# Six weight transfers per turn of an expert loop issued from ScalarE's queue instead of SyncE's

## What is computed

```python
def expert_block(args):                  # for every expert, on its tokens
    tok, e = args
    hdn = x_pad[tok] @ w1[e] + b1[e]     # 1024 -> 2 x 1024
    glu, lin = hdn[:, :D_FF], hdn[:, D_FF:]
    glu = jnp.minimum(glu, SWIGLU_LIMIT)
    lin = jnp.clip(lin, -SWIGLU_LIMIT, SWIGLU_LIMIT)
    act = glu * jax.nn.sigmoid(SWIGLU_ALPHA * glu) * (lin + 1.0)
    return act @ w2[e] + b2[e]           # 1024 -> 1024
```

## Time and profile before

| | us |
|---|---|
| median of 3 runs | 1288.67 |
| span of the profiled execution (first to last instruction) | 1287.6 |
| TensorE matmuls busy | 1224.8 (95%) |
| VectorE busy | 400.2 (31%) |
| ScalarE busy | 183.7 (14%) |
| GpSimd busy | 133.5 (10%) |

### The profile page before, as it was taken

One profiled execution on the slowest core, in us unless ns is written; L12 is line 12 of the kernel. 1 busy time (PEld: TensorE's weight loads), 2 busy tenths in 40 slices (PEclk: granted clock), 3 DMA queues, 4 the chain that ended last, 5 costly groups with the idle time before them and its releaser, 6 DMA issues.

```text
span 1287.6 us, 19010 instructions
## 1 busy us (share of the span) xinstructions
PE 1224.8 (95%) x8094; PEld 678.7 (53%) x8094; DVE 400.2 (31%) x876; ACT 183.7 (14%) x364; POOL 133.5 (10%) x125
## 2 busy tenths in 40 slices
PE   9999999999999999999999999989898989989896
PEld 8888889999864344434444443434243333324341
DVE  3869683575532121121212212021111202120213
ACT  1441621110031011101000110101010010101011
POOL 1000035788200000000000000000000000000001
PEclk9999999999999999999999999999899999999998
DMA  7745327367899999999999999999999999999995
GB/s 272 228 137 168 128 99 293 122 224 284 326 385 422 417 429 426 425 426 426 429 421 420 425 429 421 427 428 424 427 427 429 422 429 429 429 423 428 430 424 238
DMA packets 54561, 463.37 MB, mean 360 GB/s; under 512 B 12321, under 2 KB 14273, under 8 KB 19457
## 3 DMA queue, kind: packets, MB, share of 16 engines
q1 hardware_dynamic: 48576, 459.99, 87.2%
q10 hardware_dynamic: 5920, 2.45, 0.7%
HBM read 460.56 MB, written 1.87 MB: 359 GB/s over the span
## 4 chain that ended last, share of the span: by engine, by line
PE 62%; DMA 21%; SPq 3%; POOL 1%; DVE 1%; issue 1%; ACT 0%; POOLq 0%; DVEq 0%
PE ps L1215 27%; DMA mix<-expert_w 11%; DMA ring<-expert_w 10%; PE ps L1235 8%; PE ps L717 8%; PE ps L1122 4%; PE ps L1104 4%; SPq L591 3%; PE ps L740 2%; PE ps L1017 2%; PE ps L751 1%; DMA mix<-stream_w 1%; PE ps L1224 1%; PE ps L841 1%; PE ps L1208 1%
## 5 line engine op out<-in xcount | busy, mean ns | idle before, releaser
L1215 PE MATMUL ps<-ring,mix 128*64 128x512 f32 x1504 | 339.7, 596 | 8.8 <-DMA ring<-expert_w 8.7
L1215 PEld LDWEIGHTS ps<-ring,mix 128*64 128x64 f32 x1504 | 105.1, 137 | 200.4 <-issue 180.2
L1235 PE MATMUL ps<-ring,mix 128*64 128x512 f32 x752 | 172.0, 595 | 16.5 <-DMA ring<-expert_w 16.5
L1215 PE MATMUL ps<-mix 128*64 128x512 f32 x544 | 130.9, 624 | 13.2 <-DMA mix<-expert_w 13.2
L740 PE MATMUL ps<-mix 128*128 128x256 f32 x624 | 136.8, 380 | 0.0
L2244 DVE TENSOR_SCALAR mix<-ps 128x512 f32<-128x512 f32 x32 | 22.1, 691 | 353.7 <-PE ps L1215 353.7
L740 PEld LDWEIGHTS ps<-mix 128*128 128x128 f32 x624 | 117.9, 190 | 17.0 <-issue 1.2
L1235 PEld LDWEIGHTS ps<-ring,mix 128*64 128x64 f32 x752 | 51.8, 137 | 119.9 <-issue 85.4
L679 POOL TENSOR_TENSOR mix<-mix 128x1024 f32<-128x1024 f32 (+1 forms) x2 | 3.4, 1700 | 949.2 <-ACT mix L1651 949.2
L717 PE MATMUL ps<-mix 128*128 128x128 f32 x792 | 97.0, 276 | 0.3 <-POOL mix L651 0.3
L717 PEld LDWEIGHTS ps<-mix 128*128 128x128 f32 x792 | 92.1, 192 | 1.1 <-POOL mix L651 0.5
(11 more groups left out here) (297 smaller groups left out, 986.5 us busy)
## 6 DMA issues: line engine op xcount, KB each, us to landing
ring<-expert_w SPq DMA_DIRECT2D x106, 2048.0 KB, 30.5
mix<-expert_w SPq DMA_DIRECT2D x39, 2048.0 KB, 27.1
ring<-expert_w SPq DMA_DIRECT2D x70, 1024.0 KB, 24.9
mix<-stream_w SPq DMA_DIRECT2D x42, 1024.0 KB, 5.0
mix<-expert_w SPq DMA_DIRECT2D x15, 1024.0 KB, 13.9
mix<-expert_w SPq DMA_DIRECT2D x18, 512.0 KB, 24.6
mix<-stream_w SPq DMA_DIRECT2D x8, 512.0 KB, 4.3
mix<-first_w SPq DMA_DIRECT2D x4, 512.0 KB, 4.9
```

The lines of the kernel that those rows point to most:

```text
L1215: ins = mm(PS[64 * a:64 * a + 64, bank + g, :], XE[j][:, c, 64 * a:64 * a + 64], w[2 * a + g], start=start, stop=(c == KD - 1), skip_group ...
L1235: ins = mm(PS[64 * a:64 * a + 64, bank + h, :], HT[:, c // 4, c % 4, 64 * a:64 * a + 64], w[2 * h + a], start=(c == 0), stop=(c == KF - 1) ...
```

## The change

In the turns that run as a loop SyncE leaves out steps 9, 11, 13, 15, 17 and 19, and ScalarE issues them on its own queue: 9 and 11 behind the first sigmoid of the turn's first pair, 13 and 15 behind the second, 17 and 19 behind the copy of the left half. Each has the same wait on `chunk_used` as before, the same place and the same semaphore. ScalarE's loop is split like SyncE's, into one over turns 4 to 7 and one, under an If, for further rounds, since a transfer needs the number of the turn within its round. The turns that are written out are not changed.

```diff
+ACT_STEPS = ((9, 11), (13, 15), (17, 19))
@@ SyncE, load_turn
+                    if not isinstance(turn, int) and n in sum(ACT_STEPS, ()):
+                        continue
@@ ScalarE
+            def load_behind(turn, pair, part):
+
+                for n in ACT_STEPS[part]:
+                    act.wait_ge(E("chunk_used"), turn * PB * EC + STEPS * (n - SLOTS + 1))
+                    src = expert_w[bass.ds(pair + n // (EC // STEPS), 1), n % (EC // STEPS)].rearrange("e p n -> p (e n)")
+                    act.dma_start(PLACES[(n - AHEAD) % SLOTS], src).then_inc(E(f"steps_in{(n - AHEAD) % SLOTS}"), 16)
+
-            def turn_act(turn):
+            def turn_act(turn, pair=None):
                 for j in range(PB):
...
                     for f in range(2):
                         act.wait_ge(E("glu_ready"), 2 * i + f + 1)
                         A(SIG, GLU, ACT.Sigmoid, scale=SWIGLU).then_inc(E("sig_ready"), 1)
+                        if pair is not None and j == 0:
+                            load_behind(turn, pair, f)
...
                     nc_s.copy(YS[:, 0:512], PS[:, one, :]).then_inc(E("ys_left"), 1)
+                    if pair is not None and j == 0:
+                        load_behind(turn, pair, 2)
...
-            with act.Fori(STATIC, rounds * (NPAIR // PB)) as turn:
-                turn_act(turn)
+            with act.Fori(STATIC, NPAIR // PB) as q:
+                turn_act(q, q * PB)
+            with act.If(rounds > 1):
+                with act.Fori(1, rounds) as r:
+                    with act.Fori(0, NPAIR // PB) as q:
+                        turn_act(r * (NPAIR // PB) + q, q * PB)
```

## The result

Over ten executions each the changed kernel took 1291.47 us (median, 1290.71 to 1295.32) and the kernel before 1289.98 us (1288.41 to 1290.55). The ratio is 1.0018, with a 95% interval of 1.0009 to 1.0026: some 2.3 us slower, by 1.2 to 3.4 us (the two medians alone are 1.5 us apart). The forecast was +1.9.

What follows compares the result with a forecast made beforehand. DMA bytes bound the loop at 427 GB/s; even sharing of two queues ends TensorE's last turn at 115.8 us against 113.9, so 1288.67 + 1.9 = 1290.6 us. The range was 1286.0 to 1299.0.

Steps and rivals of the forecast that it cites:

- A2: Issue of steps 13 and 15 by ScalarE, 0.9 us after block 7's end, put at 48.6 us into the turn.
- Rival 1: DMA service of the two queues by whole blocks (+0.9 us, 1289.6) or in order of arrival (0); chance 0.15.
- the sum: Last turn: delayed blocks and clock loss make TensorE end at 115.8 us against 113.9, +1.9 us, thus 1290.6.
- the bound without the loss: Last turn without clock loss after waits: second issue at 46.9, block 12 at 66.7, end 117.5 us, +3.6 us.
- the floor of 114.8: Least end of the last turn, from block 8 landing at 49.0 us: 64.0 + 50.8 = 114.8, +0.9 us.
- rival 2: Two queues change the DMA rate: loss priced at 2%, 4.7 us, 1295.3, chance 0.20; gain 3.3 us, 1287.3, chance 0.08.
- Rival 3: SP's queue is the true brake in the loop; a shorter one gives back 10 us, 1280; chance 0.07.

## Why the prediction was right

**The bound.** Bytes bound the loop, as read from the share of 1.01: rate, turn length and the start of the last turn did not move. That lateness counts only in the last turn, as the prediction had it, is what the run with the change in turns 4 to 6 shows (0.9997).

**Issue times.** ScalarE's first issue in the last turn was 22.3 us into it (22.0 predicted), the second sigmoid 48.8 (A2 = 48.6). An issue took 0.344 us and not 0.32, and went out 0.2 us after the sigmoid had started and not 0.01. The address and the wait are worked out in between from the turn's number: in the run with the change in turn 7 only, where that number is a constant, the issue came 0.01 us behind the sigmoid (1184.94 against 1184.93). Nothing waited for it: behind its loop ScalarE still idles 2.08 us before its first activation, as in the earlier trace rows.

**Sharing.** An even share from 4 us after the issue was a choice made on exp_b alone; blocks 6, 7, 9, 11, 8 and 12 were put at 32.8, 42.6, 35.8, 45.6, 49.0 and 65.0 and came at 32.9, 42.7, 35.9, 45.7, 49.0 and 64.8. Rival 1 had 6 at 34.3, 7 at 44.1 and 9 at 29.4; if whole blocks alternated only from 4 us after the issue, block 6, then being moved, would have landed at 29.4 and block 9 at 34.3, which does not fit either. So rival 1 falls, and with it the reading of the Trainium skill (DMA: Bandwidth & Descriptors, Queues, rings and completion order) by which a turn between queues is as long as a whole block. That the queues take turns, as that section says, agrees with the trace. The queues' rows say something of packets after all: the 24 blocks added 3456 packets to q10 (9376 against 5920), which is 144 a block or 9 on each of the 16 engines. If the queues alternate by such packets, a turn is a ninth of a block, and that cannot be told from an even share; that they alternate so was not measured.

**The clock.** Behind the first of the two waits 16 matmuls took 5.18 us to the next start (1193.02 to 1198.20), 1.75 more than at full clock, and behind the second the row has the same 5.35; 1.7 was added for each. The granted clock agrees (columns as in the earlier trace rows): 0.83 in both stretches, so in part of each it was the lower of its two levels, 1.2 GHz and not 2.4.

```profile
1190.00:1200.00 10.00, 6.22 (x32) 2.40 (x32) 0.69 (x1) 0.00 (x0) 0.00 (x0) 0.83 1.00 428
1200.00:1210.00 10.00, 6.30 (x22) 1.93 (x24) 1.69 (x3) 0.63 (x1) 0.00 (x0) 0.83 1.01 429
```

Turn 6 of the same trace went otherwise. Block 6 lost 2.96 us (6.39 to the next start), so the wait for block 7 was only 2.35 us and block 7 ran at full speed; block 8 lost 1.5. What the sum depends on is block 7, and so this turn shows the bound without the loss:

```profile
1042.17 3.65 PE L1218 MATMUL ps<-mix 128*64 128x512 f32 x16 [0.98 <-DMA mix<-expert_w]
...
1074.60 6.57 PE L1218 MATMUL ps<-ring,mix 128*64 128x512 f32 x16 [3.81 <-DMA ring<-expert_w]
1080.99 1.04 PE L1227 MATMUL ps<-mix 128*64 128x128 f32 x16
1084.38 3.65 PE L1218 MATMUL ps<-mix 128*64 128x512 f32 x16 [2.35 <-DMA mix<-expert_w]
...
1108.86 3.65 PE L1218 MATMUL ps<-ring,mix 128*64 128x512 f32 x16 [0.95 <-DMA ring<-expert_w]
```

The second sigmoid started at 1088.81, T = 46.6 (46.9 in that bound), and block 12 came at 66.7 (66.7). A faster TensorE there makes ScalarE issue sooner and the pair end later. If the last turn of an execution goes like turn 6, it ends 2 us later; that would suit the wider spread of the changed kernel (4.6 us against 2.1), but is only argued. That this term came out right was in part luck. The prediction took 1.7 from one wait; in the same trace the wait of 3.37 us at 923.47 was followed by 6.35 us to the next start, 2.9 more than at full clock. By the prediction's own working such a loss at block 7 would have ended the turn at the floor of 114.8 (an estimate), and no loss at 117.5.

**The rivals.** No loss or gain of rate (rival 2): 428 to 431 GB/s in the first 80 us of the last turn and 422 in the next 20, where the kernel before has 419 to 433 over the same 100 us. Rival 3: SP's issue stalls did shrink, as this row of tile expert_w shows against the earlier trace rows, and gave nothing back; the Trainium skill's rule that spreading transfers over issuing engines does not help bandwidth (same page, Rules for kernel authors) holds here, with 427 GB/s before and after.

```profile
L594 SPq DMA_DIRECT2D mix<-expert_w x24: 327/594/4242, 443.5 to 1248.2; - x24
```

**What was off.** The sum was set on the median of three runs, 1288.67; over ten runs the kernel before has 1289.98. The profiled execution of the changed kernel took 1290.71 us at a span of 1288.8, so 1.9 us lie outside the span, not the 1.1 that I took. So 1290.6 came near the measured 1291.47 from a base that was 1.3 us too low. The predicted difference, +1.9, stands against +1.6 at the last chunk of the fastest execution and +2.3 (1.2 to 3.4) in the times. The landings foreseen for ScalarE's blocks, 14 to 24 us, left out the last one (28.2 us), though the sum had it. The waits of about 4 us in each loop turn were not there in every turn (2.35 for block 7 in turn 6), nor was a wait of about 1 us at each start (0.98 in turn 6, none in turn 7). And 0.40 for slower against 0.50 for no change hung on an edge: the measured ratio lies just inside 0.2%, and its interval on both sides of it.

## What to carry to other kernels

When the DMA engines are full, as here at 427 GB/s, what the choice of an issuing queue decides is the order of service. The second queue added no bandwidth; it let its transfers pass those of the first, at half the rate each. So what is needed next should not stand in the queue that is passed. A late issue in a single deep queue was harmless here, an early one on a second queue was not. Lateness of the consumer (here TensorE) was paid once, at the end of the stream, since it had slack to catch up before; so place such changes away from the last turn, or judge them by that turn alone.

## What the runs showed of the hardware

Two queues with 2 MB transfers (16 KB on each of 128 partitions) shared the 16 DMA engines so evenly that blocks of one queue landed 9.8 us apart where alone they take 4.9, with no loss of total rate (427 GB/s). The first block that ScalarE issued beside a full SP queue landed 13.7 to 14.0 us after its issue in the last turn of all six kernels that issue there, which puts the start of its share at 3.9 to 4.2 us if it moves at half rate throughout. The early stretch of the earlier trace rows, 378 GB/s beside ScalarE's first loads, says nothing on such transfers.

The clock after a wait was less regular than the sum assumed. Behind a wait of 3.4 to 3.9 us the rows of the next 16 matmuls give 5.07 to 6.57 us, where they give 3.65 at full clock. But the wait of 3.93 us at 1222.91 with steps 13 and 15 alone cost nothing (3.65 in its row, granted clock 1.00 from 1222.9 to 1226.4), and one of 2.36 us at 1160.34 with steps 9 and 11 alone did (5.35, granted clock 0.67 from 1160.3 to 1165.5), while one of 2.35 us in turn 6 of the changed kernel did not. The length of a wait alone does not say whether the clock falls, or for how long.
